# Six reorderings on VectorE in a two-layer hybrid decoder step: the up step's fourth sum, samples' copies, residuals, keys, and the form of a factor

## The reference, cut to what matters

```python
def trunk_layer(x, ...):
    h = jnp.einsum('btd,de->bte', x, w_in)
    z_u = gelu(h[..., :o1]);  z_v = layer_norm(gelu(h[..., o1:o2]), gmlp_ln_g, gmlp_ln_b)
    q = rotary(h[..., o2:o3], pos);  k = rotary(h[..., o3:o4], pos);  v = h[..., o4:]
    # prompt: 128-row blocks, each against itself and the block before;
    # samples: against 128 cached keys and values and their own 8
    attn = sink_attention(q, k_band, v_band, q_pos, k_pos, attn_sinks)
    gmlp_out = z_u * chunk_spatial(z_v, w_spatial, b_spatial)
    mix = jnp.einsum('bte,ed->btd', concat(gmlp_out, attn), w_out)
    x = layer_norm(DEEPNORM_ALPHA * x + mix, ln1_g, ln1_b)
    up = jnp.einsum('btd,df->btf', x, w_up)                 # 1024 -> 5632
    hc = conv_b + sum(conv_w[i] * hp[:, i:i + T] for i in range(3))
    g, u = hc[..., :D_FF], hc[..., D_FF:]                   # D_FF = 2816
    y = jnp.einsum('btf,fd->btd', gelu(g) * u, w_down)
    return layer_norm(DEEPNORM_ALPHA * x + y, ln2_g, ln2_b), new_k, new_v, new_conv, z_v
```

## Time and profile before

| | |
|---|---|
| time of three runs, median (lowest, highest) | 2400.87 us (2397.77, 2401.16) |
| the profiled execution: time, span | 2398.07 us, 2396.3 us |
| busy in the span: PE, DVE, ACT, POOL | 94%, 69%, 41%, 33% |
| mean granted clock of PE | 0.977 |

### The profile page before, as it was taken

The page is one execution under the profiler, slowest core; times in us unless marked ns, Lnnn a source line. Parts: engine busy times, 40 slices in busy tenths (PEclk is TensorE's granted clock), DMA queues, the critical chain, the costliest instruction groups (busy, mean ns, idle before and its releaser), DMA issues.

```text
span 2396.3 us, 35859 instructions
## 1 busy us (share of the span) xinstructions
PE 2244.6 (94%) x14276; PEld 2025.5 (85%) x14276; DVE 1655.8 (69%) x2014; ACT 980.8 (41%) x1773; POOL 782.8 (33%) x444
## 2 busy tenths in 40 slices
PE   7999899799999999999999998987999999999996
PEld 7997677699999998887799876767999999987875
DVE  1558747777777776777636586486777777767777
ACT  2227634543443444333412375454344344443332
POOL 1115234434434440220311342344443444402202
PEclk9999989899999999999999999998999999999999
DMA  5412145122222224755551213541222222255762
GB/s 149 99 29 64 57 152 164 45 83 66 73 83 71 68 83 151 276 201 183 188 132 45 56 38 102 144 152 45 65 74 83 69 70 83 83 222 197 249 213 95
DMA packets 207974, 269.50 MB, mean 112 GB/s; under 512 B 31952, under 2 KB 166584, under 8 KB 207736
## 3 DMA queue, kind: packets, MB, share of 16 engines
q1 hardware_dynamic: 207808, 267.21, 36.5%
HBM read 217.39 MB, written 46.13 MB: 110 GB/s over the span
## 4 chain that ended last, share of the span: by engine, by line
PE 56%; DVE 20%; ACT 7%; issue 5%; DMA 4%; POOL 4%; SPq 2%; DVEq 0%; ACTq 0%; POOLq 0%
PE ps L2056 23%; PE ps L1770 13%; PE ps L1735 9%; PE ps L1995 3%; DMA wblk<-in_w_up 3%; DVE rl L1424 2%; POOL bl L733 2%; SPq L528 2%; DVE bnst L1252 1%; DMA wrow<-in_w_down 1%; POOL wblk L741 1%; PE ps L1795 1%; ACT bh L938 1%; PE ps L1874 1%; DVE bl L1356 1%
## 5 line engine op out<-in xcount | busy, mean ns | idle before, releaser
L2056 PE MATMUL ps<-bt,bh 128*128 128x272 f32 x3520 | 598.2, 292 | 29.9 <-issue 19.7
L2056 PEld LDWEIGHTS ps<-bt,bh 128*128 128x128 f32 x3520 | 503.5, 191 | 37.3 <-issue 25.9
L938 ACT ACTIVATE bh<-wblk 128x512 fp32r<-128x512 f32 x308 | 183.6, 624 | 542.8 <-POOL wblk L745 237.5
L2056 PE MATMUL ps<-bt,bl 128*128 128x272 f32 x1760 | 367.3, 290 | 0.0
L1356 DVE TENSOR_TENSOR bl<-wblk,bh 128x512 fp32r<-128x512 f32 x210 | 165.2, 803 | 182.2 <-ACT bh L938 182.2
L2056 PEld LDWEIGHTS ps<-bt,bl 128*128 128x128 f32 x1760 | 278.7, 191 | 0.0
L733 POOL TENSOR_TENSOR bl<-wblk,bh 128x512 fp32r<-128x512 f32 x98 | 163.3, 1669 | 310.8 <-ACT bh L938 310.8
L1770 PE MATMUL ps<-rh,ah 128*128 128x512 f32 x792 | 246.3, 392 | 14.7 <-DVE rzd L1238 6.5
L2056 PE MATMUL ps<-ba,bh 128*128 128x272 f32 x1408 | 238.4, 292 | 9.0 <-POOL bl L733 4.1
L1770 PE MATMUL ps<-rl,ah 128*128 128x512 f32 x792 | 244.1, 389 | 0.0
L1424 DVE TENSOR_TENSOR rl<-wrow,rh 128x1024 fp32r<-128x1024 f32 x132 | 191.6, 1452 | 51.0 <-ACT rh L994 51.0
(11 more groups left out here) (223 smaller groups left out, 4081.4 us busy)
## 6 DMA issues: line engine op xcount, KB each, us to landing
wrow<-in_w_down SPq DMA_DIRECT2D x132, 512.0 KB, 4.7
wblk<-in_w_up SPq DMA_DIRECT2D x88, 512.0 KB, 5.2
a_scr<-hg SPq DMA_DIRECT2D x44, 552.0 KB, 3.4
araw<-a_scr SPq DMA_DIRECT2D x88, 192.0 KB, 4.5
wrow<-in_w_out SPq DMA_DIRECT2D x48, 256.0 KB, 5.5
wrow<-in_w_out SPq DMA_DIRECT2D x24, 512.0 KB, 4.0
wraw<-in_w_in SPq DMA_DIRECT2D x10, 1024.0 KB, 6.0
z_scr<-rzc SPq DMA_DIRECT2D x16, 512.0 KB, 3.7
```

Source lines behind the costliest of these rows:

```text
L938: act.activation(bh[b][:], block_of(f, b), ACT.Copy).then_inc(S["u_hi"], 1)
L2056: e = nc.tensor.matmul(out[:, n, :], lhs, rhs[:, HW_ // 2 * n:HW_ // 2 * n + HW_ // 2], start=(k == 0 and m == 0), stop=(k == HK - 1 and m ...
```

## The change

It moves instructions on DVE at five places, gives one another form, and lowers three wait counts that go with it. Nothing is computed otherwise, and no engine gets more or fewer instructions. In the changed kernel the lines behind 1267 have a number one lower, from the keys on others again.

```diff
-        vnew = at("vnew", [DS, DB, P], a_off + 4352)
+        vnew = [at("vnew0", [DS, 4, P], a_off + 16896), at("vnew1", [DS, 4, P], a_off + 4352)]
...
-                    act.wait_ge(S["c_done"], l * NTOK + 3)
+                    act.wait_ge(S["c_done"], l * NTOK + 1)
                 act.activation(m_part(op, 0), mix[:, k0:k1, ...], ACT.Copy).then_inc(S["m_hi"], 1)
...
-                    dve.scalar_tensor_tensor(out=nmr[0:q, i, :], in0=mv[0:q, i, 0:1], scalar=-1.0, in1=rst[0:q, i, :],
-                                             op0=ALU.mult, op1=ALU.mult).then_inc(S["ln_nm"], 1)
+                    dve.tensor_scalar(nmr[0:q, i, :], mv[0:q, i, 0:1], rst[0:q, i, :], -1.0, ALU.mult, ALU.mult).then_inc(S["ln_nm"], 1)
...
-                    if b == 5:
-                        keys()
+                    if 4 <= b < 7:
+                        keys(b - 4)          # one of the three operations each
...
                 gate(1)
+                dve.wait_ge(S["pe_pv"], (l + 1) * NB)
+                dve.tensor_copy(kcT[:, :, P:P + DS], hT[:, T_K, SEQ:T]...).then_inc(sd, 1)
+                dve.wait_ge(S["s_pe"], 6 * l + 1)
+                dve.wait_ge(S["q_rot"], 3 * (l + 1) * NB)
+                dve.tensor_copy(kvs[:], ps[0:NS, 6, 0:2 * P]).then_inc(sd, 1)
+                dve.tensor_copy(vnew[0][:], ps[0:DS, 7, :]...).then_inc(sd, 1)
                 m_lo(l, 1)
...
                     moments(l, 0, t1)
-                    joined_rz(l, 0, t2)
                     if g == 0:
                         m_lo(l, 5)
+                    joined_rz(l, 0, t2)
...
                     joined(l, f, "u2")
-                    if not last:
-                        block_lo(l, f + 1, B_S2)
                     joined(l, f, "v")
                     if f:
                         product(l, f - 1)
                     if not last:
+                        block_lo(l, f + 1, B_S2)
                         block_lo(l, f + 1, B_S1)
...
                     if k == FT - 1:
                         summed(l, 1, 3 * g)
                         summed(l, 1, 3 * g + 1)
+                        joined_rz(l, 1, 3 * g + 2)
                     act_lo(l, d + 2)
                     down_lo(l, d + 3)
...
                     if k == FT - 1:
-                        summed(l, 1, 3 * g + 2)
+                        moments(l, 1, 3 * g + 2)
...
                 def samp_turn2():
-                    pe.wait_ge(S["s_dve"], 18 * l + 6)
+                    pe.wait_ge(S["s_dve"], 18 * l + 3)
```

More of the change, by code:

```diff
@@ L1507, in gm, with keys @@
                     e.then_inc(gd, 1)
-                def keys():
-                    dve.wait_ge(S["k_sw"], 64 * (l + 1))
-                    dve.wait_ge(S["cs_landed"], 32 * (l + 1))
+                def keys(step):
                     kT = hT[:, T_K, :]
[L1513 to L1516, removed]
+                    if step == 0:
+                        dve.wait_ge(S["k_sw"], 64 * (l + 1))
+                        dve.wait_ge(S["cs_landed"], 32 * (l + 1))
+                        dve.tensor_tensor(kT, kT, cosT[:], ALU.mult).then_inc(S["k_rot"], 1)
+                    elif step == 1:
+                        dve.tensor_tensor(swk[:], swk[:], sinT[:], ALU.mult).then_inc(S["k_rot"], 1)
+                    else:
+                        dve.wait_ge(S["k_rot"], 3 * l + 2)
+                        dve.tensor_tensor(kT, kT, swk[:], ALU.add).then_inc(S["k_rot"], 1)
                 gm(0, 1)
@@ L1581, in body @@
                 gate(1)
+                sd = S["s_dve"]
+                dve.wait_ge(S["pe_pv"], (l + 1) * NB)
+                dve.tensor_copy(kcT[:, :, P:P + DS], hT[:, T_K, SEQ:T].rearrange("p (b t) -> p b t", t=DS)).then_inc(sd, 1)
+                dve.wait_ge(S["s_pe"], 6 * l + 1)
+                dve.wait_ge(S["q_rot"], 3 * (l + 1) * NB)
+                dve.tensor_copy(kvs[:], ps[0:NS, 6, 0:2 * P]).then_inc(sd, 1)
+                dve.tensor_copy(vnew[0][:], ps[0:DS, 7, :].rearrange("p (j d) -> p j d", d=P)).then_inc(sd, 1)
                 m_lo(l, 1)
-                sd = S["s_dve"]
                 qs = qr[0][:, 0:2, :].rearrange("p a c -> p (a c)").rearrange("p (b j t) -> p j b t", j=4, t=DS)
@@ L1591, in s_after @@
                     dve.wait_ge(S["s_dve"], 18 * l + k)
-                dve.wait_ge(S["pe_pv"], (l + 1) * NB)
-                dve.tensor_copy(kcT[:, :, P:P + DS], hT[:, T_K, SEQ:T].rearrange("p (b t) -> p b t", t=DS)).then_inc(sd, 1)
                 dve.wait_ge(S["q_sw0"], (l * 5 + 5) * 64)
@@ L1602, in body @@
                     .then_inc(sd, 1)
-                s_after(3)
+                s_after(5)
                 dve.tensor_tensor(qs, qs, seqs(swq[0][:, :, 0:NS]), ALU.add).then_inc(sd, 1)
[L1605 to L1608, removed]
                 dve.wait_ge(S["s_pe"], 6 * l + 2)
-                dve.tensor_copy(vnew[:, 4:8, :], ps[0:DS, 6, :].rearrange("p (j d) -> p j d", d=P)).then_inc(sd, 1)
+                dve.tensor_copy(vnew[1][:], ps[0:DS, 6, :].rearrange("p (j d) -> p j d", d=P)).then_inc(sd, 1)
                 dve.tensor_copy(kcT[:, 0:4, 0:P], ps[:, 7, :].rearrange("p (j s) -> p j s", s=P)).then_inc(sd, 1)
@@ L1644, in body @@
                     moments(l, 0, t1)
-                    joined_rz(l, 0, t2)
                     if g == 0:
                         m_lo(l, 5)
-                    elif g == 2:
+                    joined_rz(l, 0, t2)
+                    if g == 2:
                         scaled(l, 0, t1)
@@ L1976, in samp_values @@
                             nc.tensor.matmul(out, vc[:, b, o:o + 64], pTs[:, b // 2, 32 * u:32 * u + 32], start=True, stop=False)
-                            e = nc.tensor.matmul(out, vnew[:, b, o:o + 64], pTn[:, b // 2, 32 * u:32 * u + 32], start=False, stop=True)
+                            e = nc.tensor.matmul(out, vnew[b // 4][:, b % 4, o:o + 64], pTn[:, b // 2, 32 * u:32 * u + 32], start=False, stop=True)
                     e.then_inc(sp_, 1)
```

## The result

The changed kernel takes 2337.93 us (median of 4 runs, 2335.85 to 2340.51) where the kernel before took 2399.32 beside it. The ratio is 0.9746, with a 95% interval of 0.9729 to 0.9763: 61 us less, 57 to 65. I had forecast 2357 and a range down to 2343. The direction was right, and the gain was 18 us larger than said.

A forecast was written before the change was run, and what follows sets the result against it. PE, busy 94%, was taken as the bound, with its waits for DVE; -28 - 6.5 - 7 - 5.5 + 1.4 + 1.8 = -43.8 from 2398.07 gives 2354.3, 2357 with 2.8 for the median; range 2345 to 2368 (chance 0.7).

The forecast's parts named there:

- The factor's form: Line 1267 as TENSOR_SCALAR: held 2.08 us by POOL before PE's hT waits; half the gain taken, -5.5 (0 to -11).
- Up steps: Sum v and product ahead of the split of S2: 14 us a layer less, -28 in all, lower bound -35.
- collision: In up steps, product beside POOL's sum, both using SBUF: charged 1.07 us, and 0.85 on every second, longer step.
- Rival 1: In up steps a link stays untouched, longer steps keep 22.70 us: total 2370 to 2373, 2378 with factor held; chance 0.2.
- Rival 2: In up steps product delays both POOL sums by 1.3 us each: +31, total 2416, slower; chance 0.05.
- First step: First up step: PE's 2.27 us gap and 1.7 of low clock, 3.9 in all; 2.5 taken as gained.
- m_lo(5): Put ahead of the third residual, it delays moments and factor: +0.9 us a layer, +1.8 in all (0 to +2.4).
- Residual: Last down step of a group: third residual ahead of al and rl ends four PE waits, -6.5 us (-5 to -7).
- Samples: Three copies ahead of m_lo(1): PE's vnew gap falls to 3.3 us, ended by vc; -7 in all (0 to -13).
- Rival 3: At the samples the moved copies do nothing, PE waiting until 294 for another input: total 2364 us; chance 0.1.
- Keys: Three key operations spread over blocks 4, 5, 6: +0.7 us a layer, +1.4 in all (-3.8 to +4).
- the ring: Up-step dependency loop through POOL's sums, ACT's high parts, DVE's split and queue, and ACT's moves; claimed to set the step's pace.

The follow-up runs named there:

- up order alone: The kernel before with only v and the product moved ahead of the split of S2 in the up step: 2367.45 beside 2395.68 us, ratio 0.9882.

## Why the prediction was wrong where it was wrong, step by step

- **The factor's form** is the step that failed. The prediction said "Two rows are near ... so I take half, **-5.5**, and keep 0 and -11". It measured 18. Two mistakes are in it. Of the two rows the size decided, not the operation: the new form on one element took 206 to 216 ns in all 18, and from two elements on it was held. And the upper bound of 11 was the idle time of PE alone. That part was sized well (11.3 less idle time in the norms), but the low clock around these gaps was put at nothing, though the same prediction counts it behind the first up step's gap and at the samples; it measured 6.5 in this pair of executions, 3.9 in the mean of all. The first mistake costs 5.5, the second 7: 12.5 of the 18 to 19 us by which the forecast missed. Putting 18 in place of 5.5 in the sum gives 2344.5, barely inside the range.
- The rule drawn on from the Trainium skill (VectorE: DVE Perf Modes, section What auto-detection actually checks), "even or equal", would have made this part 0. With two and with three elements the runs agree with it. With one, 206 to 216 ns, they don't. The section speaks of the outermost non-unit dimensions; one element has none, so to read "one to one is equal" as covered was the prediction's own step, and the measurement decides.
- **Up steps** came out in size and, where the order stands alone, by the mechanism forecast: -28 forecast, 28 measured alone. The prediction had 21.4 a step; the 17 steps give 21.35 in "up order alone" (363.0 in all) and 21.39 in layer 1 of the changed kernel, whose longest steps are 21.75 (21.70 forecast) and whose collision is the one charged (1.17 for 1.07). In layer 0 it was missed: product started behind 745, met 749, and PE's own pace was reached in full (361.6 where I expected about 364). The mean was closer than its working. Every second step was taken at 22.70, though these take 21.9 to 22.7 (from the start times of before), and the short ones were let fall to 21.05, below PE's 21.27; the two slips work against each other. The Trainium skill's exclusion (SBUF — State Buffer, section Who interferes with whom) agrees with each order seen: an instruction that starts beside a running one of the other engine takes 1.8 to 2.5 us instead of 1.29. Rival 1 fell: no step is over 21.75. Rival 2 fell as a price: product holds one urgent sum by 1.17 in most steps, not two by 2.6, and the step still gains 0.7.
- **First step.** The 2.27 went, with a part of the clock: 3.3 where I took 2.5. In the changed kernel c22 was late next in layer 0 (1.9), a wait that I hadn't named: it stands behind both splits, and it is mostly m_lo(5)'s doing (0.5 with m_lo(5) put back).
- **Residual.** The four waits went, as said. But 6.5 was forecast, and the down stages give 2.8 in the changed kernel and 5.3 alone: 1.9 a place, less 0.7 a layer at the next wait for `ah`, less what low clock later took.
- **Samples.** -3.5 a layer forecast, -3.5 measured, ended by `vc` at a gap of 3.4 to 3.5 (3.3 said). Rival 3 fell: the next input was late by what the landing of `vc` said.
- **Keys.** +0.7 a layer forecast, 0.0 measured in layer 0. Block 4's gap is 1.44 (0.34 before) and block 5's 1.91 went, as said; the third operation met POOL (3.38), but left a gap of 0.82 and not 1.4, since its block had more slack than I gave it.
- **m_lo(5).** +0.9 a layer forecast, +1.0 to 1.1 measured.
- What remains of the miss is about 6 us. By the table, 6.9 came at places that the change doesn't touch (2.3, 3.0 and 1.6, the first loads and the low clock told above). Another 2.1 came in the up steps and 1.4 at the keys, and the residual took 3.7 back. This is read from one pair of profiled executions. The medians of several runs are 61 us apart as well, so it isn't shown that those 6.9 are chance alone; the cause stays open.

## What to carry to other kernels

When a short instruction is held by another engine, count every wait at the end of a chain in which it stands, whatever name that wait bears in the list; "line waited for" names the last link only. To each such gap belongs a price for the low clock around it, here a third to a half of the gap itself (3.9 on 12.4 in the mean, 6.5 on 11.3 in one pair). When two instructions can move into an idle gap, the one that collides with nobody (here v) gives its full length, the other what is left after the instruction of the other engine that it holds. Which one it meets can change from layer to layer of one execution, so look at both. An instruction that is moved ahead of a wait is worth what leaves the queue behind that wait, per turn of the ring, until PE's own pace is reached.

## What the runs showed of the hardware that I had not expected

- A TENSOR_SCALAR from SBUF to SBUF in float32 on one element a row was not held while GpSimd worked (216 ns at most in 18), on two and on three it was (up to 2097 and 2089 ns). The SCALAR_TENSOR_TENSOR with two SBUF inputs was held with one element already (2086).
- A hold is passed on: a product of 1.29 us held by a POOL sum takes 1.82, and the next POOL sum of 1.29 then takes 2.16, 1.4 us of holding from one meeting. Started 0.01 us from each other, product takes 1.30 and the sum 2.46. Either shows as busy time, POOL's 783 us becoming 826 with the same instructions.
- The startup and the clock's low stretches move PE by 1.5 to 3 us between executions of kernels that are the same there; an edit's worth is better read from the start times of equal PE instructions than from one total.
